# Two transformer blocks on one core: the ends of three stages taken bank by bank, and two norms in a row made as one

## The chip, the cores and the metric

The kernel runs on one core of one Trainium2 chip. The metric is the device time of one execution in microseconds; a lower one is better. The core has five engines with instruction streams of their own: TensorE (PE) for matmuls, VectorE (DVE), ScalarE (ACT), GpSimd (POOL) and SyncE (SP), which here only issues DMAs. They wait for each other by semaphores. A wait stands in an engine's own stream, so everything behind it on that engine waits too.

## The reference

All data are float32, for 256 tokens with 1024 features. The first block is a gated mixer, a cross attention and a mixture of 16 experts (MoE), and ends in a norm. The second block has two layers: layer 0 with a sparse attention, layer 1 with a differential attention, each followed by an MLP of width 4096, with shifts, scales and gates made from a condition. What matters here:

```
def rmsnorm(x, g):  return x * rsqrt(mean(x * x) + EPS) * g       # EPS = 1e-6

x = x + hierarchical_moe(rmsnorm(x, norm_ffn_g), ...)
x = rmsnorm(x, norm_f_g)                                          # "f", end of block one
h = rms_norm(x, ln_mix_g[0]) * (1 + sc1) + sh1                    # "n", layer 0
x = x + g1 * nsa_mixer(h, ...)
h = rms_norm(x, ln_mlp_g[0]) * (1 + sc2) + sh2                    # "m0"
x = x + g2 * (square(relu(h @ w_mlp_in[0])) @ w_mlp_out[0])
h = rms_norm(x, ln_mix_g[1]) * (1 + sc1) + sh1                    # "d", layer 1
x = x + g1 * diff_mixer(h, ...)
x = x + g2 * mlp(rms_norm(x, ln_mlp_g[1]) * (1 + sc2) + sh2)      # "m1", the output
```

Norm n is taken of the result of norm f, so with r the inverse root of f its mean square is r² · mean(x² g²).

## The kernel before

Everything is kept transposed: features on the 128 partitions in 8 blocks, the 256 tokens along the free axis (`x_t`, `h_hi`, `h_lo`). All large weights come in panels of 1 MB, in one order for the whole program (`plan`; `PN[name]` is a stage's first panel). SyncE loads a panel into one of two `raw` buffers. ScalarE makes its rounded high half `w_hi`, VectorE the rest `w_lo` (`ahead` on either engine does this for all panels up to three beyond the one named; four pairs of buffers). A panel's raw buffer is free once its low half is made, its split buffers once TensorE has read it (`panel_done`). Each product is three matmuls (high by high, low by high, high by low; `linear`, `down`). The order of all work on each engine is written out by hand.

`linear` writes to a ring of four PSUM banks, taken in turn by numbered fills (`FL`); who empties a bank signals `drained`. The MoE and the MLPs sum over experts or chunks in four other banks, `acc0` to `acc3`, two blocks of features in each. `down` adds one panel to them, block by block, 48 matmuls. The last one ends the sum, and VectorE then adds the banks to `x_t` (L2085 behind the MoE, L2336 behind an MLP, in `mlp`), having waited for the whole panel, and signals `moe_added` or `mlp_added`.

A norm goes like this. ScalarE squares `x_t` in four pieces (`squares_of`, L1209, which ends with a small Sqrt activation so that the table is there early). TensorE multiplies the squares with a matrix of ones (`stats`), which puts the sum over all features on every partition. Such a float32 matmul appears as two records in the trace. ScalarE takes the root (`root`), VectorE the reciprocal (`inverse`, L1676) and scales `x_t` (`split_norm`, L1707); ScalarE makes `h_hi` (`high_parts`), VectorE `h_lo` (L1701), two blocks at a time; TensorE begins the next panel with the first two. Meanwhile `keep_busy` runs matmuls of an identity whose results nobody reads.

Behind the MoE two such norms stand in a row. VectorE and ScalarE first bring the next stage's fourth panel into halves (`ahead(PN["n_q"])`). ScalarE squares `x_t`, then squares it again with the gain `f_g`; TensorE sums both; VectorE makes the reciprocal of f, multiplies the second sums with it twice (L2093, L2095, signal `n_mean`). ScalarE has meanwhile issued six DMAs for layer 0 (L1439 to L1444: weights for the compression and the token positions) and takes the second root; VectorE makes a reciprocal again (L2099), a product (L2100), and scales. Behind this VectorE scales `x_t` itself by norm f (L2103) and makes the rotation angles from the positions (L2111 to L2121), for which ScalarE waits with its sines before it empties the first `n_q` bank. GpSimd issues the loads of `w_ada` (L599) during the MoE and the first MLP, each waiting for the use of an earlier one.

Behind the first MLP VectorE also makes two dot products for a scalar lambda, and ScalarE takes their exponentials (another table) and issues a table's load (L1593), in front of the squares of norm d.

At the end TensorE turns `x_t` back (L1199), VectorE copies four banks to SBUF (L2421), SyncE stores them.

Of the kernel before, what the change touches and what calls it, by code (L numbers as in the profile page):

```python
# [23 lines left out]
I32 = mybir.dt.int32  # L24
ALU = mybir.AluOpType
# [3 lines left out]
P = 128  # L29
T = 256  # L30
# [230 lines left out]
def program(nc, a, out):  # L261
# [5 lines left out]
    with ctx:  # L267
# [9 lines left out]
        def shared(name):  # L277

            tag, _, what = name.partition("_")
            if tag not in NORMS or what not in PER_NORM:  # L280
                return name, 0
            before = [t for t in NORMS[:NORMS.index(tag)] if not (t == "f" and what in ("scaled", "hi", "ready"))]
            return "norm_" + what, PER_NORM[what] * len(before)
# [36 lines left out]
        eps = sb("eps", [P, 1])  # L320
        router_w = sb("router_w", [P, KB, 20])
# [40 lines left out]
        ADA, GATE_ROWS, SQ_N, HID_T, ADA_RAW = 0, 24, 24, 40, 54  # L362
# [179 lines left out]
        def _(pool):  # L542
# [4 lines left out]
            nc.gpsimd.memset(zero_b[:], 0.0).then_inc(S("pads"), 1)  # L547

# [73 lines left out]
            ada_loads(0)  # L622

# [6 lines left out]
        def _(pe):  # L630
# [235 lines left out]
            def down(p, slot, last_one=False):  # L866
# [4 lines left out]
                for b in range(KB):  # L871
                    o = acc[b // 2][:, (b % 2) * T:(b % 2 + 1) * T]
                    c = slice(b * P, (b + 1) * P)
                    for k in range(2):
# [3 lines left out]
                        last = mm(o, wl[:, k, c], e_hi[:, i, :], False, last_one and k == 1, skip_group_check=True)  # L878
                last.then_inc(S("panel_done"), 1)
# [35 lines left out]
            stats("f", lambda k: blk(SQX, 8)[:, k], "f_squared")  # L915
            stats("n", lambda k: blk(SQ_N, 8)[:, k], "n_squared")


            keep_busy(FL["n_q"], 21)
# [284 lines left out]
        def _(act):  # L1204
# [47 lines left out]
            def norm_act(tag, ready, shift=None, before=None):  # L1252

                squares_of(tag, x_t[:], blk(SQX, 8), ready, before)
                root(tag)
                high_parts(tag, h_hi, blk(SQX, 8), shift)
# [170 lines left out]
            ahead(PN["n_q"])  # L1427
            squares_of("f", x_t[:], blk(SQX, 8), lambda j: act.wait_ge(S("moe_added"), j + 1))

            for b in range(KB):  # L1430
                last = func(blk(SQ_N, 8)[:, b], x_t[:, b, :], ACT.Square, scale=vcol("f_g", b))
                if b % 2:
                    last.then_inc(S("n_squared"), 1)
            root("f")

            act.wait_ge(S("mod_turned"), TURNS)
            ck1, cv1 = a["nsa_w_ck1_2"][0], a["nsa_w_cv1_2"][0]
            for at, w in ((CK1, ck1), (CV1, cv1)):
                act.dma_start(flat(at, 0, 2048).rearrange("p (j h) -> p j h", j=16), w.rearrange("(j p) h -> p j h", p=P))\  # L1439
                   .then_inc(S("ck_landed"), 16)  # L1440
            for c in (0, HD):
                act.dma_start(flat(CK2, c, HD), a["nsa_w_ck2_2"][0]).then_inc(S("ck_landed"), 16)
            act.dma_start(flat(CK2, P, HD), a["nsa_w_cv2_2"][0]).then_inc(S("ck_landed"), 16)
            act.dma_start(flat(ROPE_C, 0, T).bitcast(I32), a["positions_2"].to_broadcast([P, T])).then_inc(S("pos_landed"), 16)  # L1444
            act.wait_ge(S("n_mean"), 1)
            func(norm[:, 1, :], norm[:, 0, :], ACT.Sqrt, bias=eps[:]).then_inc(S("n_root_made"), 1)
            high_parts("n", h_hi, blk(SQX, 8), lambda b: mods[:, 0, b:b + 1])

# [139 lines left out]
            ahead(PN["d_q"])  # L1588
            act.wait_ge(S("lam_dots"), 1)
            func(lam[:, 0:2], lam[:, 0:2], ACT.Exp).then_inc(S("lam_exp"), 1)  # L1590
# [3 lines left out]
            norm_act("d", lambda j: act.wait_ge(S("mlp_added"), j + 1), shift=lambda b: mods[:, 1, b:b + 1])  # L1594
# [34 lines left out]

            d_exp(0)  # L1630
# [14 lines left out]
            mlp(1, "d_o")  # L1645


        @block.vector
        def _(dve):
# [23 lines left out]
            def inverse(tag):  # L1673

                drained_wait(dve, FL[tag + "_stat"])
                chain.did(nc.vector.reciprocal(norm[:, 2, :], norm[:, 1, :]))  # L1676

# [403 lines left out]
            ahead(PN["n_q"])  # L2081
            dve.wait_ge(S("panel_done"), PN["moe"] + 3 * EXPERTS)
            for k in range(4):
# [367 lines left out]
```

## Time and profile before

| | |
|---|---|
| median of 3 runs | 1523.8 us (1523.14 to 1527.52) |
| profiled execution: its own time | 1521.02 us |
| its span, first to last instruction | 1518.4 us |
| TensorE matmuls busy | 1448.5 us (95%), 11023 records |
| VectorE busy | 964.1 us (63%) |
| ScalarE busy | 627.4 us (41%) |
| GpSimd busy | 65.7 us (4%) |
| chain that ended last | PE 81%, DVE 11%, ACT 3%, issue 2%, DMA 2%, SP's queue 1% |
| mean granted TensorE clock | 0.968 |

The span is shorter than the execution's own time by what lies around the instructions. The chain is followed back from the last instruction, at each step to what released it. The clock is granted in parts of 2.4 GHz. Time that an engine off this chain saves or loses does not count by itself.

### The profile page before, as it was taken

The page shows a single profiled execution, that of the slowest core. Times are in us where ns is not written, and L with a number is a line of the kernel's source. Part 1 is how long each engine was busy: PE and PEld are TensorE (multiplying, and loading weights), DVE is VectorE, ACT ScalarE, POOL GpSimd, SP SyncE. Part 2 cuts the span into 40 slices and gives each one's busy share as a digit, 9 for nine tenths or more (in the row PEclk, how much of TensorE's full clock was granted, in tenths as well). Part 3 has the DMA queues.
Part 4 walks back from the last instruction along what each step waited for, and adds up shares of the span by engine and source line. Part 5 has one row for each costly group of instructions (what it writes and reads, how often), then busy time and mean ns, then how long its engine had stood idle before and what let it go on. Part 6 is the DMA issues. An engine that isn't in the chain of part 4 may idle for free.

```text
span 1518.4 us, 26270 instructions
## 1 busy us (share of the span) xinstructions
PE 1448.5 (95%) x11023; PEld 1367.0 (90%) x11023; DVE 964.1 (63%) x1205; ACT 627.4 (41%) x793; POOL 65.7 (4%) x111
## 2 busy tenths in 40 slices
PE   7999999999999999989998999899989998999998
PEld 6999999889999999988986578899989876899998
DVE  5679877545677667666416856788774476555453
ACT  5444453444443333444512644334444325344441
POOL 4030000000000000000000000000000000000000
PEclk9999999999999999999968999999999989999999
DMA  8555543433588887854510024999963420256551
GB/s 230 192 181 194 165 141 124 160 118 125 190 285 267 272 273 252 275 167 133 179 49 0 2 79 147 315 305 309 311 223 109 156 84 1 84 168 192 180 181 56
DMA packets 173573, 260.92 MB, mean 172 GB/s; under 512 B 5509, under 2 KB 148147, under 8 KB 173363
## 3 DMA queue, kind: packets, MB, share of 16 engines
q1 hardware_dynamic: 160890, 203.13, 41.3%
q0 software_dynamic: 10128, 51.30, 10.0%
q10 hardware_dynamic: 2472, 5.31, 1.1%
q8 instruction: 62, 1.02, 0.3%
q14 instruction: 21, 0.16, 0.0%
HBM read 258.67 MB, written 1.05 MB: 171 GB/s over the span
## 4 chain that ended last, share of the span: by engine, by line
PE 81%; DVE 11%; ACT 3%; issue 2%; DMA 2%; SPq 1%; ACTq 0%; DVEq 0%
PE ring L635 60%; PE acc L635 19%; DVE arena L1707 1%; DVE w_lo L1661 1%; ACT arena L1209 1%; ACT w_hi L1209 1%; DVE arena L1799 1%; PE acc L1045 1%; PE ring L892 1%; DVE h_lo L1701 1%; DVE norm L1676 1%; DMA raw<-in_w_mlp_in_dram 1%; DMA vec_in<-in_nsa_pe_v_dram 1%; DVE arena L2180 1%; DVE arena L2177 0%
## 5 line engine op out<-in xcount | busy, mean ns | idle before, releaser
L1661 DVE TENSOR_TENSOR w_lo<-raw,w_hi 128x2048 fp32r<-128x2048 f32 (+1 forms) x191 | 437.0, 2289 | 338.3 <-ACT w_hi L1209 338.1
L635 PE MATMUL ring<-h_hi,w_hi 128*128 128x256 f32 x2088 | 598.5, 287 | 10.6 <-DVE h_lo L1701 7.3
L635 PE MATMUL ring<-h_lo,w_hi 128*128 128x256 f32 x2088 | 592.8, 284 | 0.0
L635 PE MATMUL ring<-h_hi,w_lo 128*128 128x256 f32 x2088 | 592.6, 284 | 0.0
L1209 ACT ACTIVATE w_hi<-raw 128x2048 fp32r<-128x2048 f32 (+1 forms) x191 | 363.4, 1903 | 241.8 <-DMA raw<-in_w_mlp_out_dram 66.8
L635 PEld LDWEIGHTS ring<-h_hi,w_hi 128*128 128x128 f32 x2088 | 402.4, 193 | 18.0 <-DVE h_lo L1701 7.4
L635 PEld LDWEIGHTS ring<-h_lo,w_hi 128*128 128x128 f32 x2088 | 402.4, 193 | 0.5
L635 PEld LDWEIGHTS ring<-h_hi,w_lo 128*128 128x128 f32 x2088 | 402.2, 193 | 0.0
L635 PE MATMUL acc<-e_hi,w_hi 128*128 128x256 f32 x768 | 219.6, 286 | 2.2 <-DVE e_lo L2306 2.1
L635 PE MATMUL acc<-e_lo,w_hi 128*128 128x256 f32 x768 | 218.2, 284 | 0.0
L635 PE MATMUL acc<-e_hi,w_lo 128*128 128x256 f32 x768 | 218.1, 284 | 0.0
L1209 ACT ACTIVATE arena<-ring 128x512 f32<-128x512 f32 (+3 forms) x118 | 69.2, 589 | 308.4 <-PE ring L635 303.3
L635 PEld LDWEIGHTS acc<-e_hi,w_hi 128*128 128x128 f32 x768 | 148.2, 193 | 2.6 <-issue 2.3
L635 PEld LDWEIGHTS acc<-e_lo,w_hi 128*128 128x128 f32 x768 | 148.2, 193 | 0.0
L635 PEld LDWEIGHTS acc<-e_hi,w_lo 128*128 128x128 f32 x768 | 148.1, 193 | 0.0
L2004 DVE SCALAR_TENSOR_TENSOR arena<-arena,cond 128x1536 f32<-128x1536 f32 x56 | 101.6, 1814 | 12.3 <-DMA arena<-in_w_ada_dram 11.3
L635 PE MATMUL ring<-k_ident 128*128 128x256 f32 x324 | 79.2, 401 | 5.5 <-DMA k_ident<-in_k_ident_dram 2.9
L635 PEld LDWEIGHTS ring<-k_ident 128*128 128x128 f32 x324 | 64.6, 202 | 16.8 <-DMA k_ident<-in_k_ident_dram 2.9
L599 POOL DMA_DIRECT2D arena<-in_w_ada_dram x64 | 33.8, 529 | 948.5 <-DVE arena L2004 314.6
L635 PE MATMUL ring<-arena,k_ones 128*128 128x256 f32 x160 | 43.6, 418 | 14.8 <-ACT arena L1209 14.3
L1209 ACT ACTIVATE e_hi<-arena 128x512 fp32r<-128x512 f32 x48 | 29.9, 624 | 60.7 <-DVE arena L2031 60.6
L1799 DVE SCALAR_TENSOR_TENSOR arena<-arena,vec 128x256 f32<-128x256 f32 x120 | 54.7, 527 | 0.0
(261 smaller groups left out, 1362.6 us busy)
## 6 DMA issues: line engine op xcount, KB each, us to landing
arena<-in_w_ada_dram POOLq DMA_DIRECT2D x64, 768.0 KB, 5.8
raw<-in_w_mlp_in_dram SPq DMA_DIRECT2D x32, 1024.0 KB, 5.5
raw<-in_w_mlp_out_dram SPq DMA_DIRECT2D x32, 1024.0 KB, 5.1
raw<-in_w_in_dram SPq DMA_DIRECT2D x24, 1024.0 KB, 5.2
raw<-in_w_e_gate_dram SPq DMA_DIRECT2D x16, 1024.0 KB, 5.6
raw<-in_w_e_up_dram SPq DMA_DIRECT2D x16, 1024.0 KB, 6.4
raw<-in_w_e_down_dram SPq DMA_DIRECT2D x16, 1024.0 KB, 5.7
raw<-in_diff_w_in_dram SPq DMA_DIRECT2D x12, 1024.0 KB, 5.1
```

What stands on the lines that cost most here:

```text
L599: pool.dma_start(flat(ADA_RAW, (n % 2) * ADA_W, ADA_W), src).then_inc(S(f"ada_landed{n % 2}"), 16)
L635: return nc.tensor.matmul(dst, lhs, rhs, start=start, stop=stop, **kw)
L892: last = nc.tensor.transpose(bank(f)[:, j * P:(j + 1) * P], src, ident[:])
L1045: last = nc.tensor.transpose(dst[:, c * P:(c + 1) * P], src[:, c * P:(c + 1) * P], ident[:])
L1209: return nc.scalar.activation(dst, src, fn, **kw)
L1661: tt(w_lo[q % SPL][:, 0:n], raw[q % RAW][:, 0:n], w_hi[q % SPL][:, 0:n].bitcast(F32), ALU.subtract)\
L1676: chain.did(nc.vector.reciprocal(norm[:, 2, :], norm[:, 1, :]))
L1701: last = stt(h_lo[:, b, :], blk(mid, 8)[:, b], shift(b), h_hi[:, b, :].bitcast(F32), ALU.add, ALU.subtract)
L1707: last = stt(blk(mid, 8)[:, b], x_t[:, b, :], gain(b), norm[:, row, :], ALU.mult, ALU.mult)
L1799: chain.did(stt(y[:, b], at, w, y[:, b], ALU.mult, ALU.add))
L2004: last = stt(done_at if k == KB - 1 else so_far, piece, cond[:, k:k + 1], so_far, ALU.mult, ALU.add)
L2180: tt(dst, dst, t, ALU.add).then_inc(S(roped), 1)
```

## The change

The last panel of a sum signals `bank_summed` after each of the first three banks, and VectorE adds each bank as it is complete (`sums_wait`). This holds for the MoE and both MLPs. Behind the MoE, norm n no longer goes by the reciprocal of norm f: TensorE first sums the squares with weights f_g² + EPS (tables that GpSimd makes beforehand in `F_GAIN2`), and the root takes EPS² as its bias, so that one root and one reciprocal give the factor of both norms together. The plain sums for norm f come behind, in place of 17 of 21 filling matmuls. The second set of squares is gone. ScalarE's six DMA issues go to GpSimd, behind `moe_added`. The fourth panel's high half goes behind the root, its low half behind the scaling of `x_t`. Behind the first MLP the panel's halves and the lambda steps leave the front of norm d; the exponential goes to the front of the attention. At the end ScalarE copies two of the four banks.

```diff
+        eps_2 = sb("eps_2", [P, 1])
+        f_gain2 = sb("f_gain2", [P, KB])
...
+            nc.gpsimd.memset(eps_2[:], EPS * EPS).then_inc(S("pads"), 1)
...
+
+            fg = vec[:, 0, VEC["f_g"]:VEC["f_g"] + KB]
+            nc.gpsimd.tensor_tensor(f_gain2[:], fg, fg, ALU.mult).then_inc(S("f_gains"), 1)
+            pool.wait_ge(S("f_gains"), 1)
+            pool.wait_ge(S("act_made"), 5)
+            for b in range(KB):
+                last = nc.gpsimd.tensor_scalar(flat(F_GAIN2, b * P, P), ones[:], f_gain2[:, b:b + 1], EPS, ALU.mult, ALU.add)
+            last.then_inc(S("f_gains"), 1)
...
+            pool.wait_ge(S("mod_turned"), TURNS)
+            pool.wait_ge(S("moe_added"), 4)
+            ck1, cv1 = a["nsa_w_ck1_2"][0], a["nsa_w_cv1_2"][0]
+            for at, w in ((CK1, ck1), (CV1, cv1)):
+                pool.dma_start(flat(at, 0, 2048).rearrange("p (j h) -> p j h", j=16), w.rearrange("(j p) h -> p j h", p=P))\
+                   .then_inc(S("ck_landed"), 16)
+            for c in (0, HD):
+                pool.dma_start(flat(CK2, c, HD), a["nsa_w_ck2_2"][0]).then_inc(S("ck_landed"), 16)
+            pool.dma_start(flat(CK2, P, HD), a["nsa_w_cv2_2"][0]).then_inc(S("ck_landed"), 16)
+            pool.dma_start(flat(ROPE_C, 0, T).bitcast(I32), a["positions_2"].to_broadcast([P, T])).then_inc(S("pos_landed"), 16)
...
+                    if last_one and b % 2 and b < KB - 1:
+                        last.then_inc(S("bank_summed"), 1)
...
 
-            stats("f", lambda k: blk(SQX, 8)[:, k], "f_squared")
-            stats("n", lambda k: blk(SQ_N, 8)[:, k], "n_squared")
...
-            keep_busy(FL["n_q"], 21)
+            open_fill(FL["f_stat"])
+            open_fill(FL["n_stat"])
+            pe.wait_ge(S("f_gains"), 2)
+            for k in range(KB):
+                if k % 2 == 0:
+                    pe.wait_ge(*sig("f_squared", k // 2 + 1))
+                last = mm(bank(FL["n_stat"])[:, 0:T], flat(F_GAIN2, k * P, P), blk(SQX, 8)[:, k], k == 0, k == KB - 1)
+            last.then_inc(S("n_summed"), 1)
+            for k in range(KB):
+                last = mm(bank(FL["f_stat"])[:, 0:T], ones[:], blk(SQX, 8)[:, k], k == 0, k == KB - 1)
+            last.then_inc(S("f_summed"), 1)
...
+            keep_busy(FL["n_q"], 4)
...
-            def norm_act(tag, ready, shift=None, before=None):
+            def norm_act(tag, ready, shift=None, before=None, behind=None):
...
+                if behind is not None:
+                    ahead(behind)
...
                 expert_step(e)
+            squares_of("f", x_t[:], blk(SQX, 8), lambda j: act.wait_ge(S("moe_added"), j + 1))
...
+            act.wait_ge(*sig("n_summed", 1))
+            act.wait_ge(S("pads"), 6)
+            f = FL["n_stat"]
+            func(norm[:, 1, :], bank(f)[:, 0:T], ACT.Sqrt, scale=1.0 / D, bias=eps_2[:]).then_inc(S(f"drained{f % BANKS}"), 1)
...
-            squares_of("f", x_t[:], blk(SQX, 8), lambda j: act.wait_ge(S("moe_added"), j + 1))
...
-            for b in range(KB):
-                last = func(blk(SQ_N, 8)[:, b], x_t[:, b, :], ACT.Square, scale=vcol("f_g", b))
-                if b % 2:
-                    last.then_inc(S("n_squared"), 1)
-            root("f")
...
-            act.wait_ge(S("mod_turned"), TURNS)
-            ck1, cv1 = a["nsa_w_ck1_2"][0], a["nsa_w_cv1_2"][0]
-            for at, w in ((CK1, ck1), (CV1, cv1)):
-                act.dma_start(flat(at, 0, 2048).rearrange("p (j h) -> p j h", j=16), w.rearrange("(j p) h -> p j h", p=P))\
-                   .then_inc(S("ck_landed"), 16)
-            for c in (0, HD):
-                act.dma_start(flat(CK2, c, HD), a["nsa_w_ck2_2"][0]).then_inc(S("ck_landed"), 16)
-            act.dma_start(flat(CK2, P, HD), a["nsa_w_cv2_2"][0]).then_inc(S("ck_landed"), 16)
-            act.dma_start(flat(ROPE_C, 0, T).bitcast(I32), a["positions_2"].to_broadcast([P, T])).then_inc(S("pos_landed"), 16)
-            act.wait_ge(S("n_mean"), 1)
-            func(norm[:, 1, :], norm[:, 0, :], ACT.Sqrt, bias=eps[:]).then_inc(S("n_root_made"), 1)
...
+            act.wait_ge(*sig("f_summed", 1))
+            f = FL["f_stat"]
+            func(norm[:, 0, :], bank(f)[:, 0:T], ACT.Sqrt, scale=1.0 / D, bias=eps[:]).then_inc(S(f"drained{f % BANKS}"), 1)
+            ahead(PN["n_q"])
...
 
-            ahead(PN["d_q"])
-            act.wait_ge(S("lam_dots"), 1)
-            func(lam[:, 0:2], lam[:, 0:2], ACT.Exp).then_inc(S("lam_exp"), 1)
+            norm_act("d", lambda j: act.wait_ge(S("mlp_added"), j + 1), shift=lambda b: mods[:, 1, b:b + 1],
+                     behind=PN["d_q"])
...
-            norm_act("d", lambda j: act.wait_ge(S("mlp_added"), j + 1), shift=lambda b: mods[:, 1, b:b + 1])
...
 
+            act.wait_ge(S("lam_dots"), 1)
+            func(lam[:, 0:2], lam[:, 0:2], ACT.Exp).then_inc(S("lam_exp"), 1)
...
+            for n in (1, 3):
+                f = FL["out_t"] + n
+                act.wait_ge(S("out_turned"), n + 1)
+                func(flat(0, n * 512, 512), bank(f)[:], ACT.Copy).then_inc(S(f"drained{f % BANKS}"), 1)
...
+
+            def sums_wait(stage, k, p):
...
+                if k < 3:
+                    dve.wait_ge(S("bank_summed"), 3 * stage + k + 1)
+                else:
+                    dve.wait_ge(S("panel_done"), p + 1)
...
             modulation(0)
-            ahead(PN["n_q"])
-            dve.wait_ge(S("panel_done"), PN["moe"] + 3 * EXPERTS)
...
+                sums_wait(0, k, PN["moe"] + 3 * EXPERTS - 1)
...
-            inverse("f")
-            chain.settle()
...
-            f = FL["n_stat"]
-            dve.wait_ge(*sig("n_summed", 1))
-            drains(stt(norm[:, 0, :], bank(f)[:, 0:T], 1.0 / D, norm[:, 2, :], ALU.mult, ALU.mult), f)
-            drained_wait(dve, f)
-            tt(norm[:, 0, :], norm[:, 0, :], norm[:, 2, :], ALU.mult).then_inc(S("n_mean"), 1)
...
-            dve.wait_ge(S("n_root_made"), 1)
-            step(nc.vector.reciprocal(norm[:, 0, :], norm[:, 1, :]))
-            chain.did(tt(norm[:, 0, :], norm[:, 0, :], norm[:, 2, :], ALU.mult))
-            split_norm("n", lambda b: gain2[:, b:b + 1], lambda b: mods[:, 0, b:b + 1], row=0)
+            split_norm("n", lambda b: gain2[:, b:b + 1], lambda b: mods[:, 0, b:b + 1])
+            drained_wait(dve, FL["f_stat"])
+            step(nc.vector.reciprocal(norm[:, 1, :], norm[:, 0, :]))
...
-                last = stt(x_t[:, b, :], x_t[:, b, :], vcol("f_g", b), norm[:, 2, :], ALU.mult, ALU.mult)
+                last = stt(x_t[:, b, :], x_t[:, b, :], vcol("f_g", b), norm[:, 1, :], ALU.mult, ALU.mult)
...
-                dve.wait_ge(S("panel_done"), PN[name] + 2 * CHUNKS)
...
+                    if b % 2 == 0:
+                        sums_wait(1 + l, b // 2, PN[name] + 2 * CHUNKS - 1)
...
 
+            dve.wait_ge(S("mlp_added"), 4)
+            split_norm("d", lambda b: mod_g[:, b:b + 1], lambda b: mods[:, 1, b:b + 1])
+            ahead(PN["d_q"])
...
-            ahead(PN["d_q"])
-            dve.wait_ge(S("mlp_added"), 4)
-            split_norm("d", lambda b: mod_g[:, b:b + 1], lambda b: mods[:, 1, b:b + 1])
...
-            dve.wait_ge(S("lam_exp"), 1)
-            step(tt(lam[:, 2:3], lam[:, 1:2], lam[:, 0:1], ALU.subtract))
-            chain.did(ts(lam[:, 3:4], lam[:, 2:3], LAM_INIT, None, ALU.subtract))
...
+
+            dve.wait_ge(S("lam_exp"), 1)
+            step(tt(lam[:, 2:3], lam[:, 1:2], lam[:, 0:1], ALU.subtract))
+            step(ts(lam[:, 3:4], lam[:, 2:3], LAM_INIT, None, ALU.subtract))
...
-            for n in range(4):
+            for n in (0, 2):
```

## Rows read from the trace of the kernel before

**Rows 1.** Chain of waits, from the last MoE panel: start, us, what.
```profile
666.33 6.03 PE acc L635 x48
...
672.45 1.92 ACT w_hi L1209
...
674.39 2.29 DVE w_lo L1661
...
677.32 2.42 ACT arena L1209 x4
...
679.76 1.28 ACT L1209
...
681.25 2.54 ACT arena L1209 x7
...
692.00 1.76 DVE norm L2099
...
694.25 0.89 DVE arena L1707 x2
```

**Rows 2.** Timeline of VectorE, same stretch: start, us, what, [idle before].
```profile
670.78 0.24 DVE L2078 SCALAR_TENSOR_TENSOR mod_g<-mod,vec 128x8 f32<-128x8 f32 x2
...
676.60 2.48 DVE L2085 TENSOR_TENSOR x_t<-acc,x_t 128x512 f32<-128x512 f32 x4
...
701.13 3.25 DVE L2103 SCALAR_TENSOR_TENSOR x_t<-x_t,vec,norm 128x256 f32<-128x256 f32 x8
```

**Rows 3.** Timeline of ScalarE, same stretch.
```profile
691.46 0.51 ACT L1209 ACTIVATE norm<-norm,eps 128x256 f32<-128x256 f32 x1 [6.36 <-issue]
...
707.89 0.42 ACT L1209 ACTIVATE arena<-arena 128x256 f32<-128x256 f32 x1 [6.29 <-DVE arena L2118]
```

**Rows 4.** Timeline of TensorE, same stretch.
```profile
678.09 9.09 PE L635 MATMUL ring<-arena,k_ones 128*128 128x256 f32 x32 [5.74 <-ACT arena L1209]
...
697.13 0.36 PE L635 MATMUL ring<-h_hi,w_hi 128*128 128x256 f32 x1 [0.89 <-DVE h_lo L1701]
```

**Rows 5.** Windows: length, busy us (count) per engine, clock, DMA share, GB/s.
```profile
678.00:682.00 4.00, 3.91 (x9) 3.20 (x10) 1.07 (x2) 3.97 (x8) 0.00 (x0) 0.50 0.80 254
682.00:687.00 5.00, 5.00 (x24) 4.38 (x23) 1.75 (x1) 3.10 (x10) 0.00 (x0) 1.00 0.26 67
...
1130.40:1137.00 6.60, 6.59 (x18) 5.37 (x19) 1.01 (x1) 3.01 (x6) 0.00 (x0) 0.58 0.88 314
```

**Rows 6.** Timelines behind the first MLP: VectorE, then ScalarE, then TensorE.
```profile
1124.90 3.22 DVE L2336 SCALAR_TENSOR_TENSOR x_t<-acc,mod,x_t 128x256 f32<-128x256 f32 x8 [1.06 <-PE acc L635]
...
1139.26 1.67 DVE L1707 SCALAR_TENSOR_TENSOR arena<-x_t,mod_g,norm 128x256 f32<-128x256 f32 x4
...
1129.63 2.19 ACT L1209 ACTIVATE arena<-x_t 128x512 f32<-128x512 f32 x4 [0.19 <-issue]
...
1130.41 6.45 PE L635 MATMUL ring<-arena,k_ones 128*128 128x256 f32 x16 [5.54 <-ACT arena L1209]
```

**Rows 7.** Timeline of GpSimd: an early load, its last before 720 us.
```profile
9.93 0.92 POOL L565 DMA_DIRECT2D router_w<-in_w_rg_dram  x1
...
632.36 0.53 POOL L599 DMA_DIRECT2D arena<-in_w_ada_dram  x1 [6.14 <-DVE arena L2004]
```

**Rows 8.** Lines of GpSimd: costliest groups.
```profile
L591 POOL TENSOR_TENSOR u_pad<-arena,u_pad 128x256 f32<-128x256 f32 x4 | 5.3, 1355 | 0.1
```

**Rows 9.** DMA issues: kind, KB, us from issue to landing.
```profile
arena<-in_w_ada_dram POOLq DMA_DIRECT2D x64, 768.0 KB, 5.8
...
arena<-in_positions_dram ACTq DMA_DIRECT2D x1, 128.0 KB, 4.7
```

**Rows 10.** Timeline of the last microseconds, all engines.
```profile
1510.04 3.23 DVE L2336 SCALAR_TENSOR_TENSOR x_t<-acc,mod,x_t 128x256 f32<-128x256 f32 x8 [9.46 <-PE acc L635]
...
1513.18 2.47 DVE L2421 COPY arena<-ring 128x512 f32<-128x512 f32 x4
...
1513.89 2.12 SPq L536 DMA_DIRECT2D out_dram<-arena  x4
```

More of the change, by code:

```diff
@@ L281, in shared @@
                 return name, 0
-            before = [t for t in NORMS[:NORMS.index(tag)] if not (t == "f" and what in ("scaled", "hi", "ready"))]
+            before = [t for t in NORMS[:NORMS.index(tag)] if not (t == "f" and what in ("scaled", "hi", "ready"))
+                      and not (t == "n" and what == "squared")]
             return "norm_" + what, PER_NORM[what] * len(before)
@@ L361, in program @@
         SQX, Q, X_P, X_PT = 40, 48, 0, 4
-        ADA, GATE_ROWS, SQ_N, HID_T, ADA_RAW = 0, 24, 24, 40, 54
+        ADA, GATE_ROWS, F_GAIN2, HID_T, ADA_RAW = 0, 24, 24, 40, 54
         def x_v_fill(i):
```

## The prediction

> **What bounds the kernel now.** I read the page first. TensorE is busy for 95% of the span and the chain that ended last lies on it for 81%, VectorE for 11%, ScalarE for 3%. So VectorE and ScalarE work costs time only where TensorE has nothing to do but wait. The windows with their granted clock, the chain of waits and the timelines then show where the change touches such places. There are three: behind the mixture of experts (MoE), behind the first MLP, and the last microseconds.
>
> Behind the MoE the reader should follow the chain [rows 1]. The last panel's 48 matmuls start at 666.33 and end at about 672.35. Then ScalarE rounds the next panel's high half (1.92), VectorE makes its low half (2.29), and only then come the adds to `x_t` [rows 2] (four in 2.48, 0.61 apart), four squares (2.42), a table load with a small activation (1.5, from 679.76 to 681.25), eight more squares with the gain, and six DMA issues on ScalarE's own queue, which hold the second root back for 6.36 us [rows 3]. After it stand a reciprocal of 1.76, a multiply, and at 694.25 the scaling of h begins. `n_q` starts on TensorE at 697.13 [rows 4], 24.8 us after the last panel. TensorE idled 5.74 us at the head of this and ran 16 sum matmuls (32 records) in 9.09.
>
> Its clock fell: 0.50 granted from 678 to 682, and 1.00 from 682 to 687 [rows 5]. Behind the MLP it was 0.58 over 6.60 us after an idle stretch of 5.54 [rows 5, 6]. A granted 0.50 is the 1.2 GHz level, 1.00 the 2.4 GHz one. One sum matmul is two records: 24 records in 5.00 us at full clock, 0.42 each; 16 records in 6.45 us, 0.81 each, behind the MLP [rows 5, 6].
>
> **The change part by part, behind the MoE.** VectorE is through with its last panel split and `modulation(0)` at 671.02 [rows 2]. The banks of the last panel are complete every 1.5 us (6.03 / 4), so by then two are. The adds run at 671.05, 671.66, 672.27, and the fourth, after the panel's end, from 672.9 to 673.55, against 679.08 before. Starting bank by bank is worth little over 1 us here; taking the 1.92 + 2.29 of panel splitting off the front is worth more.
>
> ScalarE's squares, 0.61 each, run from 671.8 to 674.2; its table load and small activation, 1.5, end at 675.7. TensorE gets its first pair at 672.4, so it has no idle stretch in front and I take the full-clock 0.42 for a sum: eight weighted sums take 3.4 and end at 675.9. The plain sums (3.4, to 679.3) and four filling matmuls (1.7, to 681.0) lie behind this, beside the reciprocal. The root is 0.51 [rows 3], to 676.45, and one reciprocal of 1.76 and no multiply [rows 1] bring the scaling of h to 678.25 against 694.25. From there to the first `n_q` matmul nothing changes: 697.13 - 694.25 = 2.9, so `n_q` starts at 681.1, just when the filling ends. **First term: 16.0 us.**
>
> What was removed has to go somewhere. The weight tables for the sums are made on GpSimd behind its last `w_ada` load of 632.36 [rows 7]. Twice the elements cost it 1.36 each there [rows 8], so eight tables need no more than 11 us, done by 644 where 672.4 is the need. I cost them at nothing. The six DMA issues leave ScalarE for GpSimd, where nothing waits behind them before `no_ready`. They begin at 673.6. An issue costs 0.53 to 0.92 there [rows 7], but the two large ones have more pieces than any in the trace: bounded by 0.53 a 128 pieces, they cost 8.5 each. I take 1.3 (nearest the row of 0.92), which has all issued by 679. The positions are small (4.7 us to landing on the other queue) and wait at most behind 2 MB; at 768 KB in 5.8 us [rows 9] that is 16 us, to 690.
>
> The Trainium skill, page "SBUF — State Buffer", section "SBUF: two separate sides", warns of just this move: VectorE instructions in the fast two-port mode keep GpSimd from writing descriptors for the DMAs that it issues. No row of this stretch has such an issue beside VectorE work. If the rule bit, the reciprocal at most would hold the issue for 1.8 us, which the slack below covers.
>
> The panel split now comes later on VectorE: h's scaling and low parts to 685.1 (701.13 - 694.25 = 6.9 behind the scaling's start), then the plain reciprocal (1.76) and the eight `x_t` scalings (3.25) to 690.2, then the low half of the fourth `n_q` panel to 692.5, then the angles. TensorE wants that panel at 681.1 + 3 x 5.8 = 698.5, at the earliest. The first sine was 3.5 us behind `x_t` [rows 2, 3]; now it comes at 696.0. Behind it on ScalarE stand the sines (0.42 each), a copy and squares (0.6 each), and the fifth panel's high half, 1.92; VectorE's low half ends at 702.3. TensorE wants this one at 681.1 + 24 = 705. So about 3 us of slack is left. The raw buffer of the sixth panel is handed back at 692.5 and a panel lands in some 5 to 6 us, still in front of its turn. Cost nothing, bounds 0 and 3.
>
> **Behind the first MLP.** VectorE is free at 1124.90 - 1.06 = 1123.84 [rows 6] with three banks complete; the adds take 0.8 a pair and end at 1127.05 against 1128.1. That is 1 us. The larger part: ScalarE's high half of 1.92, the load of the table for Exp and the exponential leave the front of the squares, which began at 1129.63 [rows 6] and now follow each add, from 1124.7 to 1127.75. TensorE starts summing at 1125.3 instead of 1130.41, idle for 0.4 us and not 5.5, so at 0.42: through at 1128.7. The table load for the root, 1.5, which lay hidden behind slow sums, is now what ends last, at 1129.2. Root 0.51, reciprocal 1.76: scaling of h at 1131.5 against 1139.26. **Second term: 7.7 us.** The panel's high half (1.92) lies beside the reciprocal; the eleven filling matmuls (4.6) end at 1133.3, 1 us before h is ready. The lambda steps move to the attention, where the Exp table is loaded ahead of scores anyhow: nothing.
>
> **The end.** VectorE idles 9.46 us in front of its last adds [rows 10], so three of the four pairs go under the panel. Adds end at 1510.85 against 1513.27, and the first two transposes are done by then. First copy at 1510.9 against 1513.18: 2.3. Two of four copies go to ScalarE beside VectorE's; the stores, back to back for 2.12 before too, take little of that. **Third term: 2.3 us**, bounds 1.5 and 3.5 (two copies of 0.6 more).
>
> **Sum.** 16.0 + 7.7 + 2.3 = 26.0 us of the profiled execution, whose span is 1518.4 and its own time 1521.0. I expect 1492.4 and 1495.0 there. The median of the runs shown is 1523.8, 2.8 above that execution, so the forecast is 1523.8 - 26.0 = 1497.8.
>
> **Rivals.**
> *The clock falls all the same.* Filling behind the MoE goes from 21 matmuls to 4. For it: both seams show that a break of 5.5 us brought 0.50. Against it: the breaks left are below 1 us. If it falls, the eight sums on the path cost 8 x (0.81 - 0.42) = 3.1 more, at each of two seams: 6.2, so 1504. If it also stays down into the first panel, the sums, fills and about as much again double: 7 at each seam, 1512. The Trainium skill, page "TensorE: Matmul & The Clock Gate", section "Why this matters for your kernels", wants bursts without idle breaks for full clock; the trace agrees at both seams, and by it cutting the fill is harmless only if no break grows.
> *GpSimd's queue is late, and it ends slower.* If the positions land behind 692.5, the angles, the sines behind them and every `n_q` bank that ScalarE drains move with them; from 3 us past that, TensorE stands. At 8.5 an issue (upper bound) they are issued at about 693 and land at 697.5: a loss of 2, time 1500. To lose all 26 us and come out slower they would have to land behind 722, some 48 us after GpSimd began, and at 727 the time would be about 1529. Only a stall of the software queue does that; 64 `w_ada` loads have a median of 5.8.
> *The seams give nothing.* If a later place had its own pace, the early start would be waited off and 1521 to 1524 remain. For it: the attention's window is bound by VectorE and ScalarE. Against it: those too start from `n_q`, and the loads from splits of panels, so nothing has a clock of its own.
> *The gain behind the MoE is partly lost* in the panels' splits (slack of 3 overdrawn, a landing of 8 to 10 us): 2 to 6 us, 1500 to 1504.
>
> **How the numbers follow.** Forecast 0.78 (its own range 1494 to 1501); the clock 0.08; split or queue overdrawn, still faster 0.09; the seams give nothing 0.03; slower 0.02. The range leaves out less than 2 in 10: from 1492, the terms' upper ends and the spread between runs, to 1506, past the first price of the clock rival. 0.3% is 4.6 us, about what a measurement can tell from no change. Faster by more 0.95, within 0.03, slower 0.02.
>
> **What the profile after would show.** Scaling of h some 6 us behind the last MoE panel and `n_q` at about 681; granted clock 1.00 through both seams; sum matmuls of 0.42; no panel wait of TensorE in `n_q` to `n_vc`; the scaling in front of `d_q` at 1131.5 - 16.0 = 1115.5; span 1492. The forecast is wrong if the clock drops in front of `n_q`, if the first sine comes after 699, or if TensorE waits for the low half of the fifth panel.

## The result, and the profile after

The changed kernel took 1507.3 us in the median of four runs (1499.8 to 1511.5), the kernel before 1525.7 (1523.1 to 1528.9, four runs): a ratio of 0.9872 with a 95% interval of 0.9845 to 0.9899, 15 to 24 us. It is faster, as forecast, but the median lies 1.3 us above the stated range, and 9.5 above the forecast of 1497.8. The profiled execution took 1499.8, its span is 1498.2 against 1518.4: 20.2 less, where 26.0 was forecast. The page's line of the chain shows the balance of engines as it was (TensorE 82%, VectorE 11%).

The chain of waits from the last MoE panel, which answers to [rows 1]:

```profile
666.12 6.01 PE acc L658 x48
...
672.21 7.16 PE ring L658 x32
...
679.39 0.48 ACT norm L1242
...
679.89 1.77 DVE norm L1706
...
681.68 0.89 DVE arena L1744 x2
...
682.60 0.92 ACT h_hi L1242 x2
...
683.54 0.89 DVE h_lo L1738 x2
```

Panel splits, adds, squares, table and DMA issues are gone from it, as forecast. But between the panel and the root stand 32 records, both groups of sums, not the 16 of the weighted ones. The timelines of TensorE, ScalarE and VectorE there, against [rows 2 to 4]:

```profile
672.21 3.69 PE L658 MATMUL ring<-arena 128*128 128x256 f32 x16
675.74 3.62 PE L658 MATMUL ring<-arena,k_ones 128*128 128x256 f32 x16
679.19 1.89 PE L658 MATMUL ring<-k_ident 128*128 128x256 f32 x8
```

```profile
671.43 2.43 ACT L1242 ACTIVATE arena<-x_t 128x512 f32<-128x512 f32 x4 [3.36 <-DVE x_t L2121]
...
679.39 0.47 ACT L1242 ACTIVATE norm<-ring,eps 128x256 f32<-128x256 f32 x1 [4.02 <-PE ring L658]
...
699.14 0.42 ACT L1242 ACTIVATE arena<-arena 128x256 f32<-128x256 f32 x1 [9.74 <-DVE arena L2144]
```

```profile
670.71 2.48 DVE L2121 TENSOR_TENSOR x_t<-acc,x_t 128x512 f32<-128x512 f32 x4
...
679.89 1.75 DVE L1706 RECIPROCAL norm<-norm 128x256 f32<-128x256 f32 x1 [6.50 <-ACT norm L1242]
...
681.68 1.67 DVE L1744 SCALAR_TENSOR_TENSOR arena<-x_t,gain,norm 128x256 f32<-128x256 f32 x4
```

The weighted sums end at about 675.8, where 675.9 was forecast, but ScalarE's root waits to 679.39, 4.02 us idle. The scaling of h begins at 681.68, not at 678.25. The filling ends at 681.1 and `n_q` starts at 684.57, so TensorE has the break of 3.5 us there that the forecast said it would not have, and its clock falls once more, as the second of these windows shows (columns as in [rows 5]: length, busy us and count of PE, PEld, DVE, ACT and POOL, then granted clock, DMA share, GB/s); the third is behind the MLP, where it stays up:

```profile
680.00:684.00 4.00, 1.08 (x5) 0.60 (x4) 3.78 (x7) 3.06 (x5) 0.00 (x0) 1.00 1.02 282
684.00:690.00 6.00, 5.43 (x28) 4.86 (x29) 5.81 (x13) 3.77 (x7) 0.00 (x0) 0.72 0.05 13
1115.00:1119.00 4.00, 3.98 (x20) 3.37 (x20) 1.78 (x5) 2.12 (x6) 0.00 (x0) 1.00 0.68 235
```

Behind the MLP, against [rows 6], the chain reads:

```profile
1109.21 6.01 PE acc L658 x48
...
1115.24 3.71 PE ring L658 x16
...
1118.97 0.48 ACT norm L1242
...
1119.54 1.77 DVE norm L1706
...
1121.33 0.89 DVE arena L1744 x2
```

The table load that the forecast put last there has gone. ScalarE's timeline of the kernel before has it between the last square and the small Sqrt activation; in the changed kernel that activation follows the squares at once, and the root waits for TensorE's sums alone:

```profile
1131.84 1.28 ACT L1209 ACT_TABLE_LOAD   x1
```

```profile
1117.35 0.19 ACT L1242 ACTIVATE note<-k_ones 128x1 f32<-128x1 f32 x1
1118.97 0.47 ACT L1242 ACTIVATE norm<-ring,eps 128x256 f32<-128x256 f32 x1 [1.43 <-PE ring L658]
```

And the end, against [rows 10]:

```profile
1492.17 0.88 DVE L2363 SCALAR_TENSOR_TENSOR x_t<-acc,mod,x_t 128x256 f32<-128x256 f32 x2 [0.56 <-PE acc L658]
1492.96 0.68 DVE L2448 COPY arena<-ring 128x512 f32<-128x512 f32 x1
...
1493.67 1.83 SPq L539 DMA_DIRECT2D out_dram<-arena  x4
```

Only one pair of adds is left behind the last panel. The first copy comes 0.8 us behind the start of that pair where it was 3.14 (in the kernel before all four pairs stood there). ScalarE's two copies run beside VectorE's.

### The profile page after: what moved, and what is told of

Same layout as the page of the kernel before. It is cut to its first block, busy times and chain, and to the rows that moved or that the text cites. A ratio compares the mean times of both kernels' runs of the same rounds, so it can differ in the third digit from the quotient of the medians.

```text
span 1498.2 us, 26200 instructions
## 1 busy us (share of the span) xinstructions
PE 1438.1 (96%) x10989; PEld 1358.3 (91%) x10989; DVE 962.0 (64%) x1200; ACT 622.8 (42%) x783; POOL 75.8 (5%) x127
## 4 chain that ended last, share of the span: by engine, by line
PE 82%; DVE 11%; ACT 3%; issue 2%; DMA 2%; POOL 0%; DVEq 0%; ACTq 0%; SPq 0%; POOLq 0%
PE ring L658 62%; PE acc L658 18%; DVE w_lo L1691 1%; ACT w_hi L1242 1%; DVE arena L1744 1%; DVE arena L1836 1%; PE acc L1078 1%; DVE norm L1706 1%; ACT arena L1242 1%; PE ring L917 1%; DVE h_lo L1738 1%; DMA raw<-in_diff_w_in_dram 1%; DMA raw<-in_w_mlp_in_dram 1%; DVE arena L2206 1%; DVE arena L2203 1%
## 5 line engine op out<-in xcount | busy, mean ns | idle before, releaser
L658 PE MATMUL ring<-k_ident 128*128 128x256 f32 x290 | 72.7, 406 | 5.4 <-DMA k_ident<-in_k_ident_dram 2.9
L658 PEld LDWEIGHTS ring<-k_ident 128*128 128x128 f32 x290 | 58.4, 204 | 16.1 <-DMA k_ident<-in_k_ident_dram 2.9
L658 PE MATMUL ring<-arena 64*128 64x256 f32 (+4 forms) x338 | 51.0, 363 | 5.5 <-ACT arena L1242 5.4
```

The lines of the kernel that those rows point to most:

```text
L658: return nc.tensor.matmul(dst, lhs, rhs, start=start, stop=stop, **kw)
```

## Experiments

The first question is why the root waits. Norms f and n count their sums on one semaphore shared by all norms (`norm_summed`), where n stands behind f. So the root's wait for "n summed" asks for the count that is reached after both groups, though TensorE now sums n's weights first. There is a reason for it in the data too: scaled h is written to the buffer of the squares (`SQX`), which the plain sums still read. **Theory A**: the root waits for both groups, at a price of one group. **Theory B**: the first group itself comes late, or something else is waited for.

The second is where the rest went: 16.0 + 7.7 + 2.3 were forecast, the three places show 12.4 + 8.3 + 2.3, which is 23.0, not 20.2. The two places behind the MoE and behind the first MLP are called seams. Their lengths, here and below, run from the start of the sum's last matmul to the start of the next stage's first, and at the end from the start of the last matmul to the end of the span.

**e0_again**: the changed kernel, unchanged.

> The changed kernel once more, unchanged, for its scatter and as the base of its neighbours. If the 20 us of the first profile are the change's and not the chip's, the scaling of h stands again about 9.8 us behind the last MoE panel's end (681.7 - 671.9), norm d again gains about 8 us and the end 2.3; what differs between profiles should lie between 760 and 1110 us, where the first profile lost 2.9 us on the kernel before. Time 1500 to 1510.

Median 1504.5 of five (1501.3 to 1507.6), the kernel before 1527.3 of eleven: a ratio of 0.9841 (0.9817 to 0.9865), 22.8 us. The profile's span is 1505.9, with the same 12.7 us behind the MoE, 9.8 behind the MLP and 6.3 at the end. One expectation failed: the two profiles of this kernel differ by 7.7 us of span, and 4.9 of them lie not between 760 and 1110 us but in the second attention, from `d_q` to `d_o`.

**e1_own_buffer**: h gets a buffer of its own, and the two waits are exchanged.

```diff
+        H_MID = 16
-            act.wait_ge(*sig("n_summed", 1))          # in front of the root of the weighted sums
+            act.wait_ge(*sig("f_summed", 1))
-            high_parts("n", h_hi, blk(SQX, 8), lambda b: mods[:, 0, b:b + 1])
-            act.wait_ge(*sig("f_summed", 1))          # in front of the root of the plain sums
+            high_parts("n", h_hi, blk(H_MID, 8), lambda b: mods[:, 0, b:b + 1])
+            act.wait_ge(*sig("n_summed", 1))
-            split_norm("n", lambda b: gain2[:, b:b + 1], lambda b: mods[:, 0, b:b + 1])
+            split_norm("n", lambda b: gain2[:, b:b + 1], lambda b: mods[:, 0, b:b + 1], mid=H_MID)
```

> Scaled h goes to blocks 16 to 23 and no longer over the squares, and ScalarE's root of the weighted sums waits for the first of the two groups of sums, the root of the plain sums for the second. Theory A (the root waits for both groups, since h is written over the squares that the plain sums read): the root starts at about 675.9 in place of 679.4, the scaling of h at 678.2 in place of 681.7, n_q on TensorE at 681.1 in place of 684.6; 3.4 us less in time, about 1 of it perhaps lost or won again in the attention. Theory B (the end of the first group comes late by itself, or the root waits for something else): the root stays at about 679.4 and the time is the changed kernel's.

The chain behind the MoE (this execution is 1.0 us later at its start):

```profile
667.08 6.02 PE acc L659 x48
...
673.17 3.71 PE ring L659 x16
...
676.90 0.48 ACT norm L1243
...
677.40 1.76 DVE norm L1707
...
679.19 0.89 DVE arena L1745 x2
```

16 records stand in front of the root in place of 32. From the last MoE matmul to the first of `n_q` it is 9.3 us against 12.7: theory A holds to a tenth, B falls. This run changes the wait and the buffer together; the wait can't be moved without the buffer, since scaled h would then overwrite squares that are still read. The median is 1502.9 of six (1497.9 to 1508.9), ratio 0.9844 (0.9817 to 0.9870); the runs' scatter is wider than 3.4 us, so the time alone (1.6 us below e0's median) does not show it.

**e2_issues_scalar**: e1 with the six DMA issues in front of the root on ScalarE's queue, and not on GpSimd.

> e1_own_buffer with the six DMA issues back on ScalarE's queue, in front of the root of the weighted sums. Theory (the issues hold the queue for about 6.4 us, as before): they begin behind the small Sqrt activation at 675.4 and the root starts at about 682 in place of 675.9; scaling of h 6 us later than in e1_own_buffer, time 6 us more. Rival (they were hidden in the kernel before, where the other sums were waited for too): less than 2 us more.

The end of this chain:

```profile
677.93 3.30 ACTq L1462
...
682.79 0.48 ACT norm L1234
```

From the last MoE matmul to `n_q` 14.4 us, 5.1 more than e1, and 0.8 more up to the gate's matmuls: 5.9 where 6 was expected. The rival falls. The median, 1505.6 of four, is only 2.7 us above e1's and lies inside the scatter; it is the place that shows the price.

**e3_fill12**: `keep_busy(FL["n_q"], 12)` for 4 in the changed kernel.

> The changed kernel with 12 filling matmuls in front of n_q in place of 4; they end at 684.6, when h is ready, so that TensorE has no idle stretch there. Theory (the half clock granted for about 3.4 us behind 685 lies under the waits for h's blocks, which come 1.6 us apart while a block pair's six matmuls take 0.7 at full and 1.4 at half clock): the clock stays at 1.00 and the time is the same within 1 us. Rival (the clock's fall costs): 1.5 to 2 us less from n_q's second panel on.

The clock stays at 1.00 from 684 to 690, where the changed kernel has 0.72:

```profile
684.00:690.00 6.00, 4.72 (x32) 3.96 (x32) 5.78 (x13) 3.46 (x6) 0.00 (x0) 1.00 0.04 10
```

`n_q` starts at the same distance (12.7), and from there to the gate's first matmul it is 59.7 us in both. The theory holds: the fall of the clock in front of `n_q` costs nothing, since the first panel waits for h's blocks anyhow. The median, 1502.4 of four, can't be told from the changed kernel's.

**e4_whole_panel**: e1, with `sums_wait` waiting for `panel_done` for every bank.

> e1_own_buffer with the adds waiting for the whole last panel at all three places, as in the kernel before. Theory (VectorE is free only shortly before the panel's end behind the MoE and the MLP, and TensorE can't begin the sums before it either, so that the bank signals are worth one add and one square there, and three of four pairs of adds at the end): last MoE matmul to n_q 9.3 becomes 10.6, behind the MLP 9.8 becomes 11.2, the end 2.4 longer; 5 us in all. Rival (the bank signals are what brought most of the gain): 10 us or more.

Behind the MoE 10.7, behind the MLP 11.0, the end 2.3 longer (8.7 from the last matmul to the span's end, 6.3 in e1, 8.7 before). 1.5 + 0.8 + 2.3 are 4.6 us: behind the MoE and at the end the bank signals are worth what was worked out, and the rival falls.

Behind the MLP the 0.8 is less sure. That seam took 9.3, 9.8, 10.2, 9.8 and 10.7 us in five profiles (the changed kernel, e0, e1, e2, e3) whose code there is the same. It goes with VectorE: its first add began 1.7, 1.1, 0.7, 1.1 and 0.2 us in front of the panel's end, since VectorE came out of the work before it earlier or later. Against e0 or e2 the bank signals are worth 1.2 there, near the expected 1.4. So a difference of less than some 1.4 us at this seam says little between two single profiles, unless the first add began equally early.

**e5_halves_front**: e1, with the fourth panel's halves in front again.

```diff
+            ahead(PN["n_q"])                    # ScalarE, before squares_of("f", ...)
+            ahead(PN["d_q"])                    # ScalarE, before norm_act("d", ...)
+            ahead(PN["n_q"])                    # VectorE, before the adds behind the MoE
```

> e1_own_buffer with the fourth panel's high and low half again in front of the adds and squares behind the MoE, and its high half in front of the squares behind the MLP. Theory: behind the MoE the sums start 1.92 + 2.29 + one add and one square, 5.5 us, later, so last MoE matmul to n_q 9.3 becomes 14.8; behind the MLP 1.92 and a square, 2.5 us, so 9.8 becomes 12.3. 8 us in all. Rival (the halves only change places, and TensorE waits for the late panel in e1_own_buffer instead): no loss here, and n_q's first panels faster by as much.

16.7 behind the MoE and 13.6 behind the MLP: 7.4 + 3.4, where 5.5 + 2.5 was expected. What is over is the clock, as the chain and the windows behind the MoE show, with TensorE's timeline behind the MoE and behind the MLP:

```profile
672.17 1.92 ACT w_hi L1243
...
674.11 2.29 DVE w_lo L1694
...
677.81 5.43 PE ring L659 x16
```

```profile
677.81 5.42 PE L659 MATMUL ring<-arena 128*128 128x256 f32 x16 [5.74 <-ACT arena L1243]
...
1123.99 5.38 PE L659 MATMUL ring<-arena,k_ones 128*128 128x256 f32 x16 [2.67 <-ACT arena L1243]
```

```profile
678.00:682.00 4.00, 4.00 (x12) 3.23 (x13) 0.96 (x3) 2.94 (x5) 2.62 (x3) 0.59 0.93 277
682.00:686.00 4.00, 4.00 (x20) 3.54 (x19) 2.19 (x3) 0.47 (x1) 1.93 (x4) 1.00 0.96 287
```

Behind the MoE TensorE idles 5.7 us, a part of the sums runs at the 1.2 GHz level (0.59 granted on the mean from 678 to 682), and the eight weighted sums take 5.43 us and not 3.71. So the halves' move is worth 5.7 there by order and another 1.7 by the clock. Behind the MLP TensorE idles 2.7 us, and its eight sums take 5.4 as well. Against e0, whose first add began as early, that seam is 3.8 longer: 2.1 by order and 1.7 by the clock. The rival, no loss, falls. Median 1512.2 of six, ratio 0.9907 (0.9875 to 0.9938).

Of the 8 us gained behind the MLP, the high half's place thus brings 3.8 and the bank signals about 1. The other 3 us stand where the table loads, the exponential and the lambda steps were; no run moves those alone.

**e6_two_norms**: the kernel before with bank signals, the later halves and the issues on GpSimd behind the MoE alone, but both norms as they were (and 14 filling matmuls for 21).

> The kernel before with the other half of what was done behind the MoE, and nothing of the rest: adds bank by bank, the panel's halves behind the second root, the six issues on GpSimd, 14 filling matmuls for 21; the two norms stay one behind the other. Worked out from rows: squares to 673.8, table to 675.3, squares with the gain to 678.6, root of f, reciprocal to 680.9, two products, root, reciprocal, product, scaling of h at 684.6, n_q at 687.4. Last MoE matmul to n_q 15.6, against 25.1 before and 9.3 in e1_own_buffer: 9.5 us for order and issues, 6.3 for the norms as one. Rival (the merged norm is most of the gain, as the issues had been hidden behind it): 20 or more. Behind the MLP 17.5 and the end as before; 9.5 us less than the kernel before.

15.6 us behind the MoE, as worked out, and the rival (20 or more) falls; 17.4 behind the MLP. What the merged norm takes away stands in this chain:

```profile
675.18 3.19 ACT arena L1222 x8
...
678.83 1.76 DVE norm L1680
...
680.61 0.43 DVE norm L2099
...
682.07 1.76 DVE norm L2105
```

So of the 15.8 us between the kernel before and e1 behind the MoE, order and issues bring 9.5 and the merge 6.3, of which the changed kernel keeps 2.8. From `n_q` to the gate e6 takes 60.4 us, where the first profile before and e1 take 59.7: 0.7 of the 9.5 is lost again there. Median 1513.7 of six, 11.6 us below the kernel before where 9.5 was expected, ratio 0.9938 (0.9905 to 0.9971).

**e8_before_look, e9_before_look**: the kernel before, twice more.

> The kernel before, unchanged, for a second profile of it. If the stretches between the seams scatter whatever the kernel, the time from the first gate matmul to n_o (133.9 in the first profile) goes with the granted clock of that stretch as in the changed kernels: 132.3 at 0.83, 133.9 at 0.82, 135.6 at 0.81, 137.3 at 0.80; and the seams themselves stay within 0.5 us at 25.1 and 17.5. If it is the change that costs there, this stretch stays at 134 and the one of the first MLP at 200.7.

> A third profile of the kernel before, unchanged, with the same expectation as for the second: seams of 25.1 and 17.5 us, and between them stretches whose length goes with the granted clock.

The seams are 26.1 and 24.9, 17.8 and 17.4: one of the four misses the expected 0.5. In that one ScalarE's queue was held 4.1 us by one DMA issue, where the first profile has 3.3. The windows from the first gate matmul to `n_o`, of the first profile before, of e8 and of e9:

```profile
756.80:890.70 133.90, 122.49 (x789) 91.18 (x787) 75.34 (x212) 53.66 (x173) 0.00 (x0) 0.82 0.06 17
```

```profile
759.60:891.70 132.10, 120.75 (x788) 88.45 (x786) 75.33 (x212) 53.63 (x173) 0.00 (x0) 0.83 0.06 17
```

```profile
756.60:894.00 137.40, 125.59 (x789) 93.73 (x787) 75.25 (x212) 53.63 (x173) 0.00 (x0) 0.80 0.05 16
```

And of the changed kernel's two profiles:

```profile
744.30:879.90 135.60, 124.02 (x788) 91.85 (x787) 75.24 (x212) 53.78 (x173) 0.00 (x0) 0.81 0.06 16
```

```profile
745.40:882.70 137.30, 125.45 (x789) 93.84 (x787) 75.23 (x212) 53.69 (x173) 0.00 (x0) 0.80 0.05 16
```

The same kernel takes 132.1 or 137.4 us for the same work, VectorE and ScalarE busy alike. The lengths of the two attention stretches go with the granted clock over all 13 profiles, and not with the kernel. That is a correlation; no run sets the clock of that stretch. It does not hold for the stretch between them: from `n_o` to the last matmul of the first MLP the 13 profiles take 232.0 to 236.4 us, the three of the kernel before 233.8 to 234.5, the two of the changed one 234.7 and 235.1, and the MLP's clock was 0.98 to 0.99 in all of them. Whether the change costs up to 1 us there stays open. The whole table (us; granted clock in brackets; from the timelines and windows of each profile):

| kernel | MoE to n_q | MLP to d_q | gate to n_o | d_q to d_o | span |
|---|---|---|---|---|---|
| before | 25.1 | 17.6 | 133.9 (0.82) | 146.6 (0.94) | 1518.4 |
| e8, before | 26.1 | 17.8 | 132.1 (0.83) | 146.6 (0.95) | 1520.3 |
| e9, before | 24.9 | 17.4 | 137.4 (0.80) | 149.9 (0.92) | 1524.8 |
| changed | 12.7 | 9.3 | 135.6 (0.81) | 146.6 (0.95) | 1498.2 |
| e0, changed | 12.7 | 9.8 | 137.3 (0.80) | 151.5 (0.91) | 1505.9 |
| e1 | 9.3 | 10.2 | 132.3 (0.83) | 149.9 (0.92) | 1496.2 |
| e2 | 14.4 | 9.8 | 135.6 (0.81) | 146.3 (0.95) | 1499.8 |
| e3 | 12.7 | 10.7 | 135.6 (0.81) | 149.3 (0.93) | 1501.7 |
| e4 | 10.7 | 11.0 | 133.5 (0.83) | 149.8 (0.92) | 1503.2 |
| e5 | 16.7 | 13.6 | 137.2 (0.80) | 150.0 (0.92) | 1511.9 |
| e6 | 15.6 | 17.4 | 135.6 (0.81) | 149.9 (0.92) | 1512.1 |
| e7 | 9.3 | 9.7 | 135.6 (0.81) | 148.3 (0.93) | 1497.8 |
| e10 | 9.3 | 8.9 | 132.3 (0.83) | 147.5 (0.94) | 1495.6 |

**e7_rounded_sums**: e1 with norm d's squares written to `h_lo`, rounded, and summed with rounded ones in one pass.

```diff
+        ones_r = sb("ones_r", [P, P], F32R)
-            stats("d", lambda k: blk(SQX, 8)[:, k], "d_squared")
+            stats("d", lambda k: h_lo[:, k, :], "d_squared", one=ones_r)
-                squares_of(tag, x_t[:], blk(SQX, 8), ready, before)
+                squares_of(tag, x_t[:], h_lo[:] if tag == "d" else blk(SQX, 8), ready, before)
```

> e1_own_buffer with norm d's squares written rounded (in h_lo's place) and summed in one pass against rounded ones, which changes that sum by its rounding. Theory (behind the MLP the full sums, 0.46 each and 3.7 in all from the panel's end, are what ends last, no longer a table load): a rounded sum costs 0.12, so the root follows the last square and comes 1.3 us earlier; last MLP matmul to d_q 9.8 becomes 8.5. Rival (something else ends last): no change.

From the last add to the scaling of h it is 3.6 us against 4.6 in e1: 0.9 of the 1.3 expected, so the full sums had indeed ended last. `d_q` hardly gains, against 8.5 expected: 9.7, where e0 and e2, whose first add began as early, have 9.8. The clock falls in this profile, the eleven filling matmuls take 6.6 us, and they run into h's time. A window and TensorE's timeline there:

```profile
1115.20:1118.00 2.80, 2.80 (x9) 2.25 (x8) 2.06 (x2) 2.27 (x2) 0.00 (x0) 0.55 0.00 0
```

```profile
1115.12 6.60 PE L661 MATMUL ring<-k_ident 128*128 128x256 f32 x22
1121.37 0.47 PE L661 MATMUL ring<-h_hi,w_hi 128*128 128x256 f32 x1
```

Median 1498.2 of five (1497.3 to 1499.5), ratio 0.9822 (0.9796 to 0.9848).

**e10_fill8**: e7 with 8 filling matmuls in front of `d_q` for 11.

> e7_rounded_sums with 8 filling matmuls for 11 in front of d_q. There the sums had become short with gaps between them, the clock fell to 0.55 between 1115.2 and 1118, and the 11 fills, 6.6 us in place of 4.9, ended 0.9 us behind the first blocks of h (1120.4). Theory: with 8 fills TensorE waits for h and d_q starts 0.9 us earlier; last MLP matmul to d_q 8.8 us. Rival (without the fills the clock stays down into d_q, whose first panel then takes longer): no gain, as its first waits end later.

8.9 us from the last MLP matmul to `d_q`, as worked out, but this does not test the eight fills. In this profile the clock stayed at 1.00, and at that level eleven (4.9 us) would have ended in front of h too: TensorE waited 1.8 us for h, as its timeline shows.

```profile
1111.91 0.47 PE L661 MATMUL ring<-h_lo,ones_r 128*128 128x256 f32 x2 [0.57 <-ACT h_lo L1245]
...
1119.96 0.35 PE L661 MATMUL ring<-h_hi,w_hi 128*128 128x256 f32 x1 [1.83 <-DVE h_lo L1741]
```

That the filling's end had held `d_q` stands in e7's own timeline. What made the clock fall in e7 is not shown either: the sums of e10 have the same gaps in front of them (0.57, 0.22, 0.28 and 0.28 us in both), and there it stayed up. Median 1497.5 of six (1496.4 to 1505.3), ratio 0.9825 (0.9797 to 0.9854): equal to e7 in time, and both medians are the lowest here. Behind the MoE both are ahead of the changed kernel; behind the MLP only e10 is.

## Why the prediction was off

**The first term, 16.0, is the step that failed.** Its sentence "The plain sums (3.4, to 679.3) and four filling matmuls (1.7, to 681.0) lie behind this, beside the reciprocal" is wrong: ScalarE's root waited for the plain sums too. The kernel showed it, in the count that `sig` makes of "n_summed" behind f's, and in the squares' buffer, which the scaled h overwrites. With the full group (3.5 measured) in front, 12.4 remains in the first profile; e1 takes it out of the way and gets 15.8 of the forecast 16.0. The rest of this term came as worked out, within half a microsecond: adds at 670.7, squares at 671.4, weighted sums to 675.8 (3.7 for the eight, where 3.4 was taken), no loss to late panels (59.7 us from `n_q` to the gate before and after), and the first sine, which counted from the panel's end is the forecast plus 3.4. So two of the forecast's own signs of being wrong appeared, the sine behind 699 (699.14) and the clock's drop in front of `n_q`, both through this step. The removal of VectorE's and ScalarE's work from the path was right, and e6 gives the split between order and merge to a tenth.

**GpSimd** was rightly costed at nothing. Its tables took 0.38 each and were done at 638.6. The six issues took 4.6 us in all, 1.2 for a large one (1.3 taken); the positions landed in 7.5 us and were there at about 686, 10 us early. The Trainium skill's warning ("SBUF — State Buffer", section "SBUF: two separate sides") had nothing to bite on, as VectorE was idle from 673.4 to 679.9.

**The second term, 7.7**, measured 8.3 and 7.7 (17.6 to 9.3 and 9.8). One step of its sum was wrong, for 0.5 us: the table load taken as what ends last is not there, as the timelines above show (without the exponential in front, nothing had taken the root's table away). The full-clock sums end last, 3.7 us in all from the panel's end in the first profile (e7 shows it by shortening them). Without the load the forecast's own sums would have ended at 1128.7, 0.5 us earlier, and the term would have been 8.2. Since this seam takes 9.3 to 10.7 us with the same code, an agreement within half a microsecond is in part luck.

**The third term, 2.3**, measured 2.3, and without the bank signals (e4) the end took 8.7 us as before, so ScalarE's two copies by themselves brought nothing.

**The clock rival** came true in part and cost nothing where it did: a break of 3.5 us in front of `n_q`, made by the failed step, brought 0.72 from 684 to 690, and e3 shows no price. Its own price, the sums at half clock, is real: e5 has it, 1.7 us a seam, with TensorE idle for 5.7 and 2.7 us in front of the sums.

**The base and the range.** Two profiles of the same kernel, before or after, differ by 6 to 8 us of span, most of it in the two attention stretches with their varying clock. The kernel before stood at 1523.8 in three runs and at 1525.3 to 1527.3 in the later medians. The first profile after lost 1.8 us in the attention, where this scatter covers it, and 1.1 up to the end of the first MLP, which stays open, against the first one before. The four runs compared came out at 18.3 us less, the next comparison, of more runs, at 22.8, which is what the three places add up to (12.7 + 8.0 + 2.3 = 23.0 with the means of all profiles of either kernel).

So the 9.5 us by which the median missed the forecast are 3.4 to 3.6 of the first term, 1.9 of a base that moved from 1523.8 to 1525.7, and about 4 that the places don't show and that the next five runs did not repeat. With the first term right the median would have been about 1503.9. But the changed kernel's next median, 1504.5, has the failed step too and lies below 1506: whether such a median falls on this or that side of 1506 is chance, while the 3.5 us of the failed step stand in all profiles with it. What sets the clock's pattern in an execution of the attention stays open.

## What to carry over

Where a change reorders two producers, look up what count their consumers wait for and whose buffer the consumer writes: a shared counter or a reused buffer turns "behind" into "in front of". At a seam the engine that waits can lose twice, by the wait and by the clock of what it does next (e5: 5.7 and 1.7 us), or only once, where what it does next waits for data anyhow (e3); so the work that feeds its first matmul goes first, and all work for later panels behind the norm's root. And take more than one profile of the kernel before when stretches outside the change can differ by more than the effect sought.

## What the runs showed of the hardware

On GpSimd the product of two 128x8 tiles took 2.28 us, in every profile that has it, and the eight operations of 128x128 behind it 0.38 each, so its time does not go with the size alone. The six DMA issues that held ScalarE's queue for 6.4 us (7.7 with the table load in e2) took GpSimd 4.6. A load of ScalarE's table took 1.28 us, and the next activation began 1.31 us behind the end of the one before. Eight full float32 sums took 3.7 us at full clock, and 5.4 to 6.5 where TensorE had idled 2.7 to 5.7 us in front of them and its clock had fallen. A stretch of the attention, with VectorE and ScalarE doing the same work, was granted 0.80 to 0.83 of the clock in different executions and took 137.4 to 132.1 us.
